# The up projections of both feed-forward blocks: each weight tile times the two halves of the rows in one product

## The reference

```python
# first block
h = rmsnorm(x, ffn_norm_w)
gate, up = split(h @ w_gate_up)            # 1024 -> 2 x 2816
x = x + (silu(gate) * up) @ w_down         # 2816 -> 1024
# second block
h = rms_norm(x, g_pre_ffn) * (1 + sc_f) + sh_f
u = causal_dwconv(h @ w_up, w_dw, b_dw)    # 3 taps over the tokens; 1024 -> 2 x 2816
val, gt = split(u)
y = (gelu(gt) * val) @ w_down              # 2816 -> 1024
```

## Time and profile before

| | us |
|---|---|
| median of 3 runs (790.93, 795.9, 794.31) | 794.31 |
| the profiled execution | 791.43 |
| its span, first to last instruction | 789.6 |
| PE busy / weight loads / DVE / ACT | 752.4 / 692.3 / 577.5 / 388.6 |

### The profile page before, as it was taken

The page is one execution under the profiler, slowest core; times in us unless marked ns, Lnnn a source line. Parts: engine busy times, 40 slices in busy tenths (PEclk is TensorE's granted clock), DMA queues, the critical chain, the costliest instruction groups (busy, mean ns, idle before and its releaser), DMA issues.

```text
span 789.6 us, 13345 instructions
## 1 busy us (share of the span) xinstructions
PE 752.4 (95%) x5290; PEld 692.3 (88%) x5290; DVE 577.5 (73%) x963; ACT 388.6 (49%) x653; POOL 30.8 (4%) x34
## 2 busy tenths in 40 slices
PE   7998999779999999999999989999999999999996
PEld 7987999767899999999979887799979899999995
DVE  5748787567766867769668998867766766766776
ACT  5472222643533544344474444458357555555644
POOL 0030000002000000000013000000000000000000
PEclk9999999999999999999999999999999999999999
DMA  7735343545279987889716632354444665455431
GB/s 291 271 104 163 104 133 109 160 133 161 84 272 409 329 295 259 280 297 335 279 54 198 204 106 81 107 214 154 155 145 154 198 197 199 161 205 193 161 135 53
DMA packets 40526, 148.94 MB, mean 189 GB/s; under 512 B 4496, under 2 KB 4624, under 8 KB 40080
## 3 DMA queue, kind: packets, MB, share of 16 engines
q1 hardware_dynamic: 39600, 142.91, 53.0%
q10 hardware_dynamic: 864, 5.18, 1.7%
HBM read 147.02 MB, written 1.05 MB: 188 GB/s over the span
## 4 chain that ended last, share of the span: by engine, by line
PE 74%; DVE 12%; ACT 7%; issue 5%; POOL 1%; DMA 1%; DVEq 0%; SPq 0%; ACTq 0%; POOLq 0%
PE bank L997 13%; PE bank L1000 13%; PE bank L998 13%; PE bank L1038 5%; PE bank L1039 5%; PE bank L1036 5%; PE bank L1014 5%; PE bank L1167 4%; DVE wlo L1394 3%; PE bank L1027 3%; DVE arena L1400 3%; ACT whi L1931 2%; ACT arena L1931 2%; DVE XN L1400 2%; ACT XN L1931 1%
## 5 line engine op out<-in xcount | busy, mean ns | idle before, releaser
L997 PE MATMUL bank<-hh,whi 128*128 128x256 f32 x1008 | 289.9, 288 | 0.7 <-DVE hl L1394 0.5
L998 PE MATMUL bank<-hl,whi 128*128 128x256 f32 x1008 | 286.2, 284 | 0.0
L1000 PE MATMUL bank<-hh,wlo 128*128 128x256 f32 x1008 | 286.1, 284 | 0.0
L1394 DVE TENSOR_TENSOR wlo<-raw,whi 128x1024 fp32r<-128x1024 f32 x202 | 244.1, 1241 | 48.6 <-ACT whi L1931 48.4
L1931 ACT ACTIVATE whi<-raw 128x1024 fp32r<-128x1024 f32 x202 | 202.4, 1047 | 28.5 <-DMA raw<-w_dram 19.8
L997 PEld LDWEIGHTS bank<-hh,whi 128*128 128x128 f32 x1008 | 194.1, 193 | 5.0 <-issue 2.9
L998 PEld LDWEIGHTS bank<-hl,whi 128*128 128x128 f32 x1008 | 194.3, 193 | 1.5
L1000 PEld LDWEIGHTS bank<-hh,wlo 128*128 128x128 f32 x1008 | 194.2, 193 | 0.0
L1400 DVE SCALAR_TENSOR_TENSOR arena<-bank,cols,arena 128x255 f32<-128x255 f32 (+3 forms) x138 | 58.9, 480 | 30.6 <-ACT arena L1931 28.4
L1931 ACT ACTIVATE arena<-bank 128x256 f32<-128x256 f32 (+2 forms) x65 | 26.9, 422 | 97.3 <-PE bank L1000 69.6
L1038 PE MATMUL bank<-wlo,fh 128*128 128x512 f32 x176 | 69.2, 393 | 1.1 <-DVE wlo L1394 1.1
(11 more groups left out here) (168 smaller groups left out, 887.5 us busy)
## 6 DMA issues: line engine op xcount, KB each, us to landing
raw<-w_dram SPq DMA_DIRECT2D x268, 512.0 KB, 4.8
arena<-rows_dram ACTq DMA_DIRECT2D x1, 1792.0 KB, 9.1
X<-x_dram SPq DMA_DIRECT2D x2, 512.0 KB, 4.9
arena<-rows_dram ACTq DMA_DIRECT2D x1, 1024.0 KB, 12.5
arena<-bias_dram ACTq DMA_DIRECT2D x1, 1024.0 KB, 15.8
out_dram<-X SPq DMA_DIRECT2D x4, 256.0 KB, 2.0
const<-const_dram ACTq DMA_DIRECT2D x1, 640.0 KB, 3.9
arena<-bias_dram ACTq DMA_DIRECT2D x1, 512.0 KB, 6.4
```

Of the source, the lines that this page charges most:

```text
L997: e.matmul(o, a, hh[:, k, :], start=(k == 0), stop=False)
L998: e.matmul(o, a, hl[:, k, :], start=False, stop=False)
L1000: ins = e.matmul(o, wlo[:, s, k * 128:k * 128 + 128], hh[:, k, :], start=False, stop=(k == 7))
L1394: return e.tensor_tensor(out, a, b, op)
```

## The change

The rows' two parts now lie side by side, `hx[:, k, 0, :]` = hh and `hx[:, k, 1, :]` = hl. A new step `wide` takes for each k one matmul of 512 columns, whi by both parts, and one of 256 columns, wlo by hh, into the left half. So each unit fills a bank of its own (sum of two products left, the third product right) and a pair takes two banks, (0, 1) or (6, 7) in turn. A pair's halves must then be added: the new step `glu_low` on ACT copies the right halves of both banks to an arena tile `sums`, and `glu_a` on DVE adds the left halves to it. `glu` is cut into the steps a to d, of which b, c and d of pair j-1 now stand among the steps of pair j. The d units come two pairs behind instead of one. The unsplit first two pairs of block 2 are kept.

```diff
 def downs(up, j):
-    if up == "w_up_2" and j < 3:
-        return (0, 1) if j == 2 else ()
-    return (j - 1,) if 0 < j <= FT - 4 else ()
+    return (j - 2,) if 1 < j <= FT - 3 else ()
...
+    def wide(n, up, j, norm):
+        for m, f in enumerate((j, FT + j)):
+            name = f"{'gu'[m]}{n}{j}"
+            P.fill(name, WIDE[(n + j + 1) % 2] + m, frees=2 - m)
+            i = P.unit("s", up, f)
+            P.of[i] = (name, norm)
+            P.step("wide", i, 0)
+            yield
+            P.step("wide", i, 1)
+            P.fills_bank(i, name)
+            yield
...
-    def ffn(n, tags, up, down, norm, norm_next, block, first):
+    def ffn(n, up, down, norm, norm_next, block):
         four_of_a(f"d{n}", 2)
         for j in range(FT):
-            if j >= 2:
-                finish(pair(f"u{n}{j}", up, (j, FT + j), ("h", norm)))
-            P.step("glu", n, j)
+            units = wide(n, up, j, norm) if n == 1 or j >= 2 else iter(())
+            next(units, None)
+            next(units, None)
+            if j:
+                P.step("glu_b", n, j - 1)
+            next(units, None)
+            next(units, None)
+            if j:
+                P.step("glu_c", n, j - 1)
+            P.step("glu_low", n, j)
+            if j:
+                P.step("glu_d", n, j - 1)
             if (n, j) == (1, 2):
                 P.step("tables")
                 P.step("biases2")
             for k in downs(up, j):
                 moving(P.unit("m", down, k), f"d{n}", k, k == 0, False, src=f"f{n}")
+            P.step("glu_a", n, j)
+        for part in "bcd":
+            P.step(f"glu_{part}", n, FT - 1)
         last_four(norm_next, f"d{n}", down, range(FT - 4, FT), f"f{n}", block)
...
+WIDE = (0, 6)
...
-        hh = sb("hh", [128, KT, T], F32R)
-        hl = sb("hl", [128, KT, T], F32R)
+        hx = sb("hx", [128, KT, 2, T], F32R)
+        hh, hl = hx[:, :, 0, :], hx[:, :, 1, :]
...
+            def wide(i, part):                      # TensorE
+                name, norm = P.of[i]
+                s = place[i] % HL
+                o = open_bank(name) if part == 0 else banks[F[name].bank]
+                w.wait_ge("hi", place[i] + 1)
+                h_ready(norm, part)
+                for k in range(4 * part, 4 * part + 4):
+                    c = slice(k * 128, k * 128 + 128)
+                    e.matmul(o, whi[:, s, c], hx[:, k, :, :], start=(k == 0), stop=False)
+                    w.wait_ge(*P.lo_on[i])
+                    ins = e.matmul(o[:, 0:256], wlo[:, s, c], hh[:, k, :], start=False, stop=(k == 7))
+                if part:
+                    filled(ins, name)
...
+            def glu_a(n, j):                        # VectorE
+                if n == 2 and j < 2:
+                    return
+                name, s = f"g{n}{j}", sums[:, j % 2, :, :]
+                wait_full(name)
+                wait_full(f"u{n}{j}")
+                w.wait_ge(F[name].e, F[name].after - 1)
+                b = F[name].bank
+                freed(tt(s, s, psum[:, b:b + 2, 0:256], ALU.add), name)
+            def glu_b(n, j):
+                if n == 1:
+                    wait_after(f"g{n}{j}")
+                    w.wait_ge("sg", j + 1)
+                    s = sil[:, j % 2, :]
+                    freed(tt(s, s, sums[:, j % 2, 1, :], ALU.mult), f"u{n}{j}")
+                    return
...                                                 # n = 2: the four taps, from sums
+            def glu_c(n, j):
+                if n == 2:
+                    c = fc[:, j % 2, :]
+                    w.wait_ge("gg", j + 1)
+                    tt(c[:, 0:256], c[:, 0:256], c[:, 256:512], ALU.mult).then_inc(sems["gm"], 1)
+            def glu_d(n, j):
+                src = sil[:, j % 2, :] if n == 1 else fc[:, j % 2, 0:256]
+                w.wait_ge(f"fh{n}", j + 1)
+                tt(fl[:, j % 4, :], src, fh[:, j % 4, :].bitcast(F32), ALU.subtract).then_inc(sems[f"fl{n}"], 1)
...
+            def glu_low(n, j):                      # ScalarE
+                if n == 2 and j < 2:
+                    return
+                name = f"g{n}{j}"
+                wait_full(name)
+                wait_full(f"u{n}{j}")
...
+                b = F[name].bank
+                freed(af(sums[:, j % 2, :, :], psum[:, b:b + 2, 256:512], ACT.Copy), name)
+            def glu_a(n, j):
+                if j >= 2:
+                    w.wait_ge(f"fl{n}", j - 1)
+                if n == 1:
+                    wait_after(f"g{n}{j}")
+                    af(sil[:, j % 2, :], sums[:, j % 2, 0, :], ACT.Silu).then_inc(sems["sg"], 1)
+                    return
...                                                 # n = 2: scale and bias of both halves, from sums
+            def glu_b(n, j):
+                if n == 2:
+                    wait_after(f"u{n}{j}")
+                    c = fc[:, j % 2, 256:512]
+                    af(c, c, ACT.Gelu_apprx_tanh).then_inc(sems["gg"], 1)
+            def glu_c(n, j):
+                if n == 1:
+                    wait_after(f"u{n}{j}")
+                    src = sil[:, j % 2, :]
+                else:
+                    w.wait_ge("gm", j + 1)
+                    src = fc[:, j % 2, 0:256]
...
                 af(fh[:, j % 4, :], src, ACT.Copy).then_inc(sems[f"fh{n}"], 1)
```

More of the change, by code:

```diff
@@ L280, in four_of_a @@
             P.fill(f"{tag}{n // 2}{n % 2}", first + n)
[L282 to L286, removed]
     def halves(norm, tags, name, fs, between):
@@ L616, in plan @@
     P.keep(6, main=True)
-    first_four(1, ("u10", "u11"), "w_gate_up", (0, FT, 1, FT + 1))
-    ffn(1, None, "w_gate_up", "w_down", 1, 2, final_block, None)
+    ffn(1, "w_gate_up", "w_down", 1, 2, final_block)
     P.step("mod_sum", 1)
-    first_four(2, ("glu0", "glu1"), "w_in_2", (12, 16, 13, 17))
+    finish(pair("glu0", "w_in_2", (12, 16), ("h", 2)))
+    P.step("glu2", 0)
+    finish(pair("glu1", "w_in_2", (13, 17), ("h", 2)))
     P.side = [4, 5, 6, 7]
@@ L749, in out2_block @@
         P.step("store", b)
-    ffn(2, None, "w_up_2", "w_down_2", 3, None, out2_block, None)
+    ffn(2, "w_up_2", "w_down_2", 3, None, out2_block)
     return P
+WIDE = (0, 6)
 FREES = {"qk": 2, "qq": 2, "gg": 2}
@@ L802, in program @@
         arena = sb("arena", [128, NAR])
-        banks = [ctx.enter_context(nc.psum_tensor(f"bank{i}", [128, 512], F32)) for i in range(8)]
+        psum = ctx.enter_context(nc.psum_tensor("bank", [128, 8, 512], F32))
+        banks = [psum[:, i, :] for i in range(8)]
         def K(name):
@@ L884, in program @@
         fc = region(0, 2, 512)
+        sums = region(11776, 2, 2, T)
         FW, GPM, GPF = region(8192, 1024), region(9216, 1024), region(10240, 1024)
@@ L1366, in _ @@
             does = {
-                "start": start, "turn": turn, "stat": stat, "whole": whole, "half": half, "movv": movv, "mov": mov, "four": four, "ba": ba,
+                "start": start, "turn": turn, "stat": stat, "wide": wide, "whole": whole, "half": half, "movv": movv, "mov": mov, "four": four, "ba": ba,
                 "turn_ba": turn_ba, "lam": lam_, "norms": norms, "decay": decay, "kk": kk, "kq": kq, "lev_first": lev_first,
@@ L1863, in co @@
                         ALU.subtract).then_inc(sems["yl"], 1)
[L1867 to L1873, removed]
+            def glu_a(n, j):
[8 more added lines that the diff above has]
+            def glu_b(n, j):
                 if n == 1:
+                    wait_after(f"g{n}{j}")
+                    w.wait_ge("sg", j + 1)
                     s = sil[:, j % 2, :]
-                    w.wait_ge("sg", j + 1)
-                    freed(tt(s, s, p[:, 256:512], ALU.mult), name)
-                    split_low(1, j, s)
+                    freed(tt(s, s, sums[:, j % 2, 1, :], ALU.mult), f"u{n}{j}")
                     return
                 c = fc[:, j % 2, :]
+                if j >= 2:
+                    wait_after(f"g{n}{j}")
+                    src = [sums[:, j % 2, m, :] for m in range(2)]
+                else:
+                    p = wait_full(f"u{n}{j}")
+                    src = [p[:, m * 256:m * 256 + 256] for m in range(2)]
                 for s in (1, 2):
@@ L1904, in _ @@
                 "glu2": glu2, "v2": v2_, "tap": tap, "mean": mean, "variance": variance, "u2": u2, "co": co, "ao": ao,
-                "glu": glu,
+                "glu_a": glu_a, "glu_b": glu_b, "glu_c": glu_c, "glu_d": glu_d,
             }
@@ L2207, in co @@
                     af(hh[:, f, :], gat[:, f, :], ACT.Copy, scale=0.5).then_inc(sems["yh"], 1)
-            def split_high(n, j, src):
+            def glu_low(n, j):
[4 more added lines that the diff above has]
+                wait_full(f"u{n}{j}")
+                if n == 2 and j < 4:
+                    w.wait_ge("yl", 8)
+                elif j >= 2:
+                    wait_after(f"u{n}{j - 2}")
+                b = F[name].bank
+                freed(af(sums[:, j % 2, :, :], psum[:, b:b + 2, 256:512], ACT.Copy), name)
```

(21 more changed lines are left out.)

10 lines of the change are left out of this document (3 added, 7 removed).

## The result

The changed kernel takes 859.66 us (median of 4 runs, 856.42 to 862.31) against 792.62 us of the kernel before, measured beside it: 8.3% slower, ratio 1.083 with a 95% interval of 1.0796 to 1.0864. The prediction was 859, range 850 to 880, slower with 0.94.

A forecast was written before the change was run, and what follows sets the result against it. PE set the pace before; the change would make the ACT and DVE chain bound block 2. 791.4 + 65.6 + 2 - 3.9 + 0.9 = 856.0 us, with 2.9 for the median 859, range 850 to 880.

The forecast's parts named there:

- The round of block 2: Block 2: ACT and DVE form one chain of 11.74 us a pair, against 8.32 us that PE needs.
- Start and end of block 2: Block 2: lo(u of 3) ready at 614.8; after 17 rounds, 7.5 us to lo(u of 21), then a 22.4 us tail.
- PE's waits for wlo: Block 2: PE waits for wlo before each unit, 0.9 to 1.5 us at a time.
- The clock in the tail: Block 2's tail: PE's stops lower the clock, adding 2 us on the last 18 matmuls.
- the three stops of 3 to 4 us: Block 2's tail: PE stands still three times, for 3 to 4 us each.
- Block 1: Block 1 stays bound by PE: 3.9 us saved over 22 pairs, 0.9 us added at its end.
- The sum: Whole kernel: the terms added to the profiled execution before, 791.4 us, give 856.0 us.
- The 2.9 us that I added for the median: Whole kernel: the median shown lay 2.9 us above the profiled execution, raising 856.0 to 859.
- rival 1: Block 2: the clock falls throughout, giving 903 us; chance 0.06.
- Rival 2: Block 1: fetch waits enter the chain in most pairs, 0.8 us in each of 18, giving 873 us; chance 0.05.
- Rival 3: Block 2: no chain, PE stays the bound at 8.32 us a pair, giving 786.3 or 789 us; chance 0.05.

The follow-up runs named there:

- e6: Changed kernel plus one unused 128x256 ACT copy behind gelu in each pair of block 2 from pair 2 on; 863.46 us.
- e7: Kernel before plus one unused 128x256 ACT copy behind gelu in block 2 from pair 2 on; 795.36 us against 794.73, ratio 0.9997.
- e10: Changed kernel with block 2's steps reordered, d 21 prepared early in block 1, four 512-column products then four of 256; 790.36 us, ratio 0.9962 to before.
- e5: Kernel before with only block 1 as in the change, block 2 as before; 791.99 us, ratio 0.9981.
- e12: e10 without the early hi and lo of d 21, which stand behind the last pair's steps again; 788.24 us, ratio 0.9948 to before.
- e11: e10 with products of 512 and 256 columns in turn instead of grouped; 794.49 us, ratio 0.9998 to before.
- e9: Changed kernel with only the matmul order in wide changed, four of 512 columns then four of 256; 855.63 us.

## Why the prediction was right, and where its terms were off

The mechanism was the one predicted, and in block 2 its size too. The terms in turn, each in its profiled execution:

- *The round of block 2*: 11.74 predicted, 11.70 measured. e6 and e7 show that it is a closed round with ACT in it, e10 that the same work in another order needs only 8.35.
- *Start and end of block 2*: from the start of scale and bias of pair 1 to lo(u of 21) 215.7 predicted, 215.1 measured (610.61 to 824.48 + 1.23 = 825.71); from there to lo(d 21) 22.4 predicted, 22.6 measured (847.05 + 1.23 = 848.28).
- *PE's waits for wlo*: predicted before each unit, 0.9 to 1.5 us at a time. They are there, but shorter: from one start to the next 0.93, 0.94 and 0.56 us in a pair are lost at wlo, and the rest of the 3.3 us at hi, in smaller pieces.
- *The clock in the tail*: +2 predicted, 0 measured. Of the three stops of 3 to 4 us that I foresaw, PE made one (3.68 us), behind one of 2.55 and one of 1.90. The granted clock did fall (0.53 from 836 to 847 us), but the matmuls that it slowed were done before lo(d 21) came, and the last 18, 0.23 us apart, ran at the upper level. I charged the clock where PE was not the bound.

```profile
836.00:847.00 11.00, 7.32 (x19) 5.30 (x19) 6.21 (x13) 5.11 (x9) 0.00 (x0) 0.53 0.01 2
```

PE's timeline there; the first product that needs lo(d 21) starts at 848.33, 0.54 us behind the one before it, so PE had to wait for lo(d 21) even here:

```profile
847.79 0.40 PE L1073 MATMUL bank<-whi,fh 128*128 128x512 f32 x1
848.33 0.50 PE L1075 MATMUL bank<-wlo,fh 128*128 128x512 f32 x1
848.67 0.40 PE L1076 MATMUL bank<-whi,fl 128*128 128x512 f32 x1
```

- *Block 1*: -3.0 predicted, +0.16 measured, a miss of 3.2 us in a small term. Three parts. A pair was 8.39 instead of 8.32 us, since a product of 512 columns and one of 256 in turn take 0.353 us and not the sum of their distances in longer rows of one kind: 22 pairs give 2.4 instead of 3.9. The late fetches around 246 us, where the tables are fetched too, reached PE: from pair 3 to pair 8 it took 43.11 us instead of 5 x 8.39, 1.2 us more. I had looked for late fetches only near the end of the block; there they cost nothing. And the tail, from PE's last product of the pairs to the square behind the block, was 1.4 us longer, not 0.9 (6.89 against 5.50).

ACT's timeline at the late fetches of the changed kernel:

```profile
243.92 0.60 ACT L1986 ACTIVATE arena<-bank 128x512 f32<-128x512 f32 x1 [0.59 <-PE bank L1037]
249.99 1.06 ACT L1986 ACTIVATE whi<-raw 128x1024 fp32r<-128x1024 f32 x1 [5.47 <-DMA raw<-w_dram]
```

- *The sum*: 856.0 on the scale of the profiled execution before. The measured difference of the stretches is 0.16 - 0.05 + 65.07 = 65.2, which gives 856.6; the changed kernel's profiled execution took 860.94, the rest being the 4.3 us ahead of block 1. The 2.9 us that I added for the median stood for just that scatter: the execution shown of before was a short one. The median before was 794.31 in the prediction's three runs and is 792.62 with a fourth, so that the difference foreseen was 64.7 us and the measured one is 67.0. So the last digit of the agreement is luck: 2 us too much for the clock and 3.2 us too little in block 1 largely cancelled.
- *The rivals*: the granted clock was 1.00 from 630 to 800 us, with PE stops of up to 1 us in each round, so rival 1 is out and the Trainium skill's account of a clock that goes to and fro with short idle times ("TensorE: Matmul & The Clock Gate", section "A second HAM failure mode: psum-queue depth-cycling") did not show here. Rival 2, block 1 chained too, is out by e5. Rival 3 is out by every row above; but PE is the bound again in e10 and e12, with another order. The Trainium skill's gap of N/2.4 + 2.5 ns for an isolated product (same page, "Back-to-back issue gap") is not met: a joined product saves 6 to 7 ns a piece (0.3594 to 0.353 us), not 2.5.

What stays open: why a product of 512 columns followed by one of 256 costs 5 ns more than the two distances, and what makes the late fetches differ between executions. e11's block 1 is 1.2 us longer than the changed kernel's, 0.87 of it in its tail, where hi and lo of d 21 stand in front, and 0.27 at the late fetches (43.38 against 43.11).

## What to carry to other kernels

When steps of one unit of work are spread among those of the next, write down the list of each engine and follow one round through both, with every wait; if the two engines never work side by side, the round's length is the sum of all their work, however low the busy shares are. Place work that is free to run (here hi and lo of the weights) where an engine would wait anyway, never between two halves of a dependent chain, and a wait for a late resource behind what others need. One more cheap instruction on the suspected engine, in both kernels, tells whether it is on the path.

## What the runs showed of the hardware

Four products of 512 columns and then four of 256 take 0.351 us a pair of products, the two in turn 0.353; both are below three of 256 (0.359), so in these kernels feeding both halves of the rows at once is worth only 2%, 0.15 us in a pair of 8.50. Ahead of block 1 the same instructions took 210.1 us in the profiled execution of the kernel before and 213.7 in that of e7, with the granted clock at the lower level for some 7 us in the first and for 17 us in the second; the changed kernel took 214.4 and e9, with the same code there, 209.8. So a difference of 4 us between two profiles there is no effect of a change.
